# A hybrid decoder trunk: queries and keys of the stick-breaking layers by products of 512 and 256 columns, one PSUM bank per head

## The chip, the core and the metric

The kernel runs as one program on one core of a Trainium2 chip. The metric is the device time of one execution in microseconds (us), the median of a few runs. Five engines work side by side and meet at semaphores: TensorE (PE; its weight loads are listed apart as PEld), VectorE (DVE), ScalarE (ACT), GpSimd (POOL) and SyncE (SP), which here only issues DMAs.

## The reference, cut to what matters

Four layers, T = 256 tokens, width 1024, 8 heads of 128; layers 0 and 3 are stick-breaking, layer 1 differential, layer 2 forgetting attention. A feed-forward net stands before and behind each attention, so there are eight.

```python
for i in range(DEPTH):
    x = x + 0.5 * swiglu(rms_norm(x, norm_g[i, 0]), ...)
    h = rms_norm(x, norm_g[i, 1])
    q, k, v = jnp.split(h @ w_qkv[i], 3, axis=-1)
    if i % 3 == 0:      # stick-breaking, per block of 128 queries
        z = q @ k.T * HEAD_DIM ** -0.5, masked strictly (SB_NEG)
        log_one_minus = log_sigmoid(-z)
        w = exp(z + log_one_minus + rev_excl_cumsum(log_one_minus))
        mix = w @ v
    ...
    x = x + mix @ w_o[i]
    x = x + 0.5 * swiglu(rms_norm(x, norm_g[i, 2]), ...)
return rms_norm(x, final_g)
```

## The kernel before, in words

**Three products for one.** A float32 product is made of three fp32r products: a value is split into a high part (a copy rounded to fp32r) and a low part (the rest). With weights W and tokens X it is W_hi X_hi + W_hi X_lo + W_lo X_hi, summed in PSUM. `product` (lines 1258 to 1262) issues these three.

**The weight stream.** Weights come in chunks of 128 x 2048. For each chunk SP loads it into one of four `raw` buffers, ACT makes the high part (`hi`, line 459, tile `w_hi`) and DVE the low part (`lo`, line 742, tile `w_lo`), both in rings of six. `split_to(c)`, on ACT and on DVE, means: do this for all chunks up to number c. PE waits for `lo_ready` of a chunk before it uses it, and a `raw` buffer is loaded again when `lo` has read it. The tokens (`xg`) are split as well: `xg[:, 0]` is the high part, `xg[:, 1]` the low part, each 8 blocks of 128 rows by 256 tokens.

**An attention layer** has four pairs of heads, j = 0 to 3. `ATT_ORDER` gives the chunks in the order of the stream: v0 v1 q0 k0 v2 v3 q1 k1 q2 k2 o0 q3 k3 o1 o2 o3. `a` is the pair whose scores are made, `b` the pair before it. Nothing schedules the work: each engine runs its own list, written out by hand, in order. For j of 1 to 3 they are these, with the names that the prediction uses:

- PE: `head_projection` of q head 0, q head 1, k head 0 (each 8 times `product`, with 256 columns, into half of a bank: q into bank 0 of `work`, k into bank 1); `mixed(b)` (line 1581 on, the later sums of the log terms); `head_projection` of k head 1; `weighted_values(b)` (line 1600 on, into bank 0); for j = 2 also `output(0)`; `scores(a)` (line 1566 on, into banks 2 and 3).
- DVE: `scale_qk` of q (line 990: PSUM times the row of norms, into `q_t`, one instruction for both heads), `log_weights(b)` (line 1007), `scale_qk` of k, `mix(b)` (line 1013, the low part of the mixed values), `mask(a)` (line 1064), `normalise(a)` (lines 1084 and 1087). Between them stand the `lo` instructions.
- ACT: `hi` instructions, `weights(b)` (lines 596 and 598, the exponentials of both heads), `mix(b)` (line 608), `exponentials(a)` (lines 640, 642, 644 and, behind line 1084 on DVE, 646).

`mixed` waits for line 1087, `weighted_values` for line 596 (head 0) and line 598 (head 1), `scores` for `scale_qk` of k. Behind the last pair PE runs `output(1)`, a quarter of `output(2)`, `mixed(3)`, a quarter of `output(2)`, `weighted_values(3)`, and the rest of the outputs. In pair 0 the value projections `values((2,))` and `values((3,))` stand where `weighted_values` stands later.

Of the kernel before, what the change touches and what calls it, by code (L numbers as in the profile page):

```python
# [14 lines left out]
P = 128  # L15
# [25 lines left out]
DMA_SCRATCH = 8192  # L41
# [7 lines left out]
KINDS = [i % 3 for i in range(DEPTH)]  # L49
LAM_INIT = 0.8 - 0.6 * math.exp(-0.3 * KINDS.index(DIFF))  # L50

# [109 lines left out]
def trunk(nc, stream, x_in, gains, consts, lam_in, subln_in, wf_in, bf_in, final_in, out):  # L161
    with ExitStack() as ctx:
# [29 lines left out]
        pair_h = sb("pair_h", [P, COLS])  # L192
        idle_in = pair_h[:, 0:P]
# [59 lines left out]
        rope_in = sem("rope_in")  # L253

# [108 lines left out]
        def slot_free(eng, c):  # L363

            if c < RING:
                return
            c -= RING
            layer, n, c0, att, no = [p for p in phases() if p[2] <= c][-1]
            what, j = (ATT_ORDER if att else FFN_ORDER)[c - c0]
            if (what, j) in (("down", UNITS - 1), ("o", PAIRS - 1)):  # L370
                eng.wait_ge(acc_ready, BANKS * (n + 1))
            elif what == "top":
                eng.wait_ge(top_used, no * len(PLAIN) + PLAIN.index(j) + 1)
            elif what == "bottom":
                eng.wait_ge(gu_psum, (no * len(PLAIN) + PLAIN.index(j)) * TB + 2)
            elif what == "down":
                eng.wait_ge(down_used, no * (UNITS - 1) + j + 1)
            elif what in PARTS:
                eng.wait_ge(part_psum, (no * len(SEVEN) + SEVEN.index(j)) * len(PARTS) + PARTS.index(what) + 1)
            elif what == "v":  # L380
                eng.wait_ge(v_psum, layer * PAIRS + j // 2 * 2 + 2)
            elif what == "o":
                eng.wait_ge(out_used, layer * (PAIRS - 1) + j + 1)
            else:
                eng.wait_ge(qk_psum, 2 * (layer * PAIRS + j) + (what == "k") + 1)
# [56 lines left out]
        def _(act):  # L442
# [114 lines left out]
            def attention(layer, n, c0, _, kind):  # L557
# [12 lines left out]
                act.preload_act_table_set("natural_log_exp_and_others")  # L570
                values(0)
                values(1)
                if layer == 0:
                    act.wait_ge(lam_psum, 1)
                    nc.scalar.activation(lam_e[:], work[:, 3, 0:2], ACT.Exp).then_inc(lam_exp, 1)
# [4 lines left out]
                if kind == FOX:  # L580

                    act.wait_ge(f_ready, 1)
                    nc.scalar.activation(fg[:, 1], fg[:, 0], ACT.Abs).then_inc(act_step, 1)
                    own_step()
                    nc.scalar.activation(fg[:, 1], fg[:, 1], ACT.Exp, scale=-1.0).then_inc(act_step, 1)
                    own_step()
                    nc.scalar.activation(fg[:, 2], fg[:, 1], ACT.Ln, bias=1.0).then_inc(f_ln, 1)
                values(2)
# [48 lines left out]
                def exponentials(a):  # L637
                    act.wait_ge(scores_ready, a + 1)
                    if kind == STICK:
# [4 lines left out]
                        nc.scalar.activation(s_c, s_b, ACT.Ln, bias=1.0).then_inc(exp_ready, 1)  # L644
                        act.wait_ge(stick_ready, KINDS[:layer].count(STICK) * PAIRS + a - first + 1)
# [9 lines left out]
                for j in range(PAIRS + 1):  # L655
                    a, b = first + j, first + j - 1
                    if j < PAIRS:
# [6 lines left out]
                    if j:  # L664
# [63 lines left out]
        def _(dve):  # L728
            split = [0]
            own = [0]  # L730

# [192 lines left out]
            def attention(layer, n, c0, _, kind):  # L924
# [62 lines left out]
                def scale_qk(dst, bank, count, scale):  # L987

                    dve.wait_ge(qk_psum, count)
# [118 lines left out]
                for j in range(PAIRS + 1):  # L1108
                    a, b = first + j, first + j - 1
                    if j < PAIRS:  # L1110
# [12 lines left out]
                        if kind == STICK or kind == DIFF and j < 2 or kind == FOX and j != 1:  # L1123
                            split_to(q_chunk + 4)
                    if kind == STICK and j in (2, 4):
                        log_weights(b)
                    if j < PAIRS:
                        scale_qk(k_t, 1, 2 * a + 2, 1.0)
# [4 lines left out]
                    if j and kind != DIFF:  # L1133
                        mix(b)
# [14 lines left out]
                    if j < PAIRS:  # L1149
# [5 lines left out]
                        elif kind != DIFF or j == 0:  # L1155
                            split_to(q_chunk + (5 if j else 6))
# [100 lines left out]
        def _(pe):  # L1257
# [227 lines left out]
            def attention(layer, n, c0, _, kind):  # L1485
# [44 lines left out]
                def head_projection(c, bank, h, between=None):  # L1530

                    pe.wait_ge(lo_ready, c + 1)
                    ins = project(work[:, bank, h * T:(h + 1) * T], c, h * P, between)
                    if h:
                        ins.then_inc(qk_psum, 1)
# [119 lines left out]
                for j in range(PAIRS):  # L1655
# [6 lines left out]
                    if not (kind == DIFF and j == 2):  # L1662
                        head_projection(c, 0, 0)
# [3 lines left out]
                    head_projection(c, 0, 1)  # L1667
# [4 lines left out]
                    head_projection(c + 1, 1, 0)  # L1672
# [12 lines left out]
                    head_projection(c + 1, 1, 1, between)  # L1685
                    if j == 0:
# [3 lines left out]
                        pe.wait_ge(qk_ready, 2 * a + 1)  # L1690
# [9 lines left out]
                    if kind != DIFF or j > 1:  # L1700
                        if kind == DIFF:
                            pe.wait_ge(rope_in, 2 * j + 1)
                        else:
# [83 lines left out]
```

## Time and profile before

| | us |
|---|---|
| median of 3 runs | 1895.06 |
| lowest and highest of them | 1894.70, 1895.39 |
| the profiled execution | 1894.82 |
| its span (first to last instruction) | 1893.0 |
| PE busy | 1878.9 (99% of the span) |
| DVE busy | 1536.3 (81%) |
| ACT busy | 1073.7 (57%) |
| granted TensorE clock, mean | 0.999 |
| DMA | 349 MB, 184 GB/s |

The span starts at 0; the attention of layer 0 lies at about 195 to 296 us and that of layer 3 at about 1603 to 1704 us. The profiled execution took 1.82 us more than its span. PE is the engine that is nearly always busy; ends of matmuls are modelled, so what counts for it is the distance from one start to the next.

### The profile page before, as it was taken

How to read it: one execution, taken by the hardware profiler on the slowest of the kernel's cores; microseconds unless marked ns; L12 is line 12 of the kernel's file. 1: busy time of each engine (PE TensorE's matmuls, PEld its weight loads, DVE VectorE, ACT ScalarE, POOL GpSimd, SP SyncE). 2: the span in 40 equal slices, each digit the busy share in tenths (PEclk: the TensorE clock that was granted, in tenths of full speed). 3: DMA queues.
4: the chain of work that ended last, by engine and by line, in shares of the span. 5: the costliest groups of instructions: out<-in, count | busy, mean ns of one | idle time of the engine just before them, and what ended most of it. 6: DMA issues, size and time to landing. Idle time of an engine off the chain costs nothing.

```text
span 1893.0 us, 22572 instructions
## 1 busy us (share of the span) xinstructions
PE 1878.9 (99%) x9408; PEld 1591.6 (84%) x9408; DVE 1536.3 (81%) x1341; ACT 1073.7 (57%) x1107; POOL 19.9 (1%) x34
## 2 busy tenths in 40 slices
PE   9999999999999999999999999999999999999998
PEld 7888998888888898788888889988888888998886
DVE  7987568987898778898799865789879987559985
ACT  6655555655565544665566553466556655556653
POOL 0000000000000000100000000000000000000000
PEclk9999999999999999999999999999999999999999
DMA  6557343456254542344625453434462545433542
GB/s 248 200 230 267 134 156 133 200 200 246 101 226 198 230 168 102 153 200 200 266 110 227 198 200 123 170 131 200 200 267 114 226 196 198 180 132 132 229 198 86
DMA packets 49893, 349.09 MB, mean 184 GB/s; under 512 B 6144, under 2 KB 6400, under 8 KB 7936
## 3 DMA queue, kind: packets, MB, share of 16 engines
q1 hardware_dynamic: 49360, 346.54, 47.2%
q8 instruction: 74, 1.21, 0.3%
q10 hardware_dynamic: 432, 1.11, 0.2%
q14 instruction: 27, 0.22, 0.0%
HBM read 346.58 MB, written 1.05 MB: 184 GB/s over the span
## 4 chain that ended last, share of the span: by engine, by line
PE 89%; DVE 7%; ACT 2%; issue 1%; DMA 0%; POOL 0%; POOLq 0%; ACTq 0%; DVEq 0%
PE work L1260 18%; PE work L1262 18%; PE work L1261 18%; PE acc L1260 10%; PE acc L1262 10%; PE acc L1261 10%; DVE w_lo L742 3%; PE work L1418 1%; PE acc L1304 1%; PE work L1462 1%; PE work L1600 1%; ACT w_hi L459 0%; PE work L1566 0%; DMA x<-x_dram 0%; PE work L1570 0%
## 5 line engine op out<-in xcount | busy, mean ns | idle before, releaser
L742 DVE TENSOR_TENSOR w_lo<-raw,w_hi 128x2048 fp32r<-128x2048 f32 x327 | 741.7, 2284 | 33.6 <-ACT w_hi L459 33.5
L459 ACT ACTIVATE w_hi<-raw 128x2048 fp32r<-128x2048 f32 x327 | 614.1, 1909 | 81.1 <-DVE raw L762 63.3
L1260 PE MATMUL work<-w_hi,xg 128*128 128x512 f32 x1040 | 411.2, 395 | 1.0 <-DVE xg L1185 1.0
L1262 PE MATMUL work<-w_hi,xg 128*128 128x512 f32 x1040 | 405.5, 390 | 0.0
L1261 PE MATMUL work<-w_lo,xg 128*128 128x512 f32 x1040 | 404.8, 389 | 0.0
L1260 PE MATMUL acc<-w_hi,m_hi 128*128 128x512 f32 x824 | 325.6, 395 | 0.2
L1262 PE MATMUL acc<-w_hi,m_lo 128*128 128x512 f32 x824 | 321.2, 390 | 0.0
L1261 PE MATMUL acc<-w_lo,m_hi 128*128 128x512 f32 x824 | 320.9, 389 | 0.0
L1262 PEld LDWEIGHTS work<-w_hi,xg 128*128 128x128 f32 x1040 | 195.3, 188 | 41.5
L1260 PEld LDWEIGHTS work<-w_hi,xg 128*128 128x128 f32 x1040 | 195.3, 188 | 39.4 <-issue 1.2
L1261 PEld LDWEIGHTS work<-w_lo,xg 128*128 128x128 f32 x1040 | 195.5, 188 | 38.4
L1262 PEld LDWEIGHTS acc<-w_hi,m_lo 128*128 128x128 f32 x824 | 154.7, 188 | 32.8
L1260 PEld LDWEIGHTS acc<-w_hi,m_hi 128*128 128x128 f32 x824 | 154.8, 188 | 31.7 <-DVE w_lo L742 1.0
L1261 PEld LDWEIGHTS acc<-w_lo,m_hi 128*128 128x128 f32 x824 | 154.9, 188 | 30.7
L742 DVE TENSOR_TENSOR w_lo<-extra,w_hi 128x2048 fp32r<-128x2048 f32 x72 | 164.2, 2281 | 0.0
L459 ACT ACTIVATE w_hi<-extra 128x2048 fp32r<-128x2048 f32 x72 | 135.3, 1913 | 46.1 <-DVE extra L755 36.7
L1262 PE MATMUL work<-w_hi,wide_r 128*128 128x512 f32 x384 | 149.8, 390 | 0.0
L1260 PE MATMUL work<-xg,w_hi 128*128 128x256 f32 x512 | 148.6, 290 | 0.6 <-DVE fg L955 0.5
L1262 PE MATMUL work<-xg,w_lo 128*128 128x256 f32 x512 | 144.7, 283 | 0.0
L1261 PE MATMUL work<-xg,w_hi 128*128 128x256 f32 x512 | 144.7, 283 | 0.0
L482 ACT ACTIVATE m_hi<-work 128x512 fp32r<-128x512 f32 x88 | 49.8, 595 | 136.3 <-PE work L1418 109.7
L806 DVE TENSOR_TENSOR m_lo<-work,m_hi 128x512 fp32r<-128x512 f32 x88 | 58.3, 686 | 67.4 <-ACT m_hi L482 67.4
(199 smaller groups left out, 2194.1 us busy)
## 6 DMA issues: line engine op xcount, KB each, us to landing
raw<-stream_dram SPq DMA_DIRECT2D x303, 1024.0 KB, 5.0
extra<-stream_dram SPq DMA_DIRECT2D x24, 1024.0 KB, 6.9
x<-x_dram SPq DMA_DIRECT2D x2, 512.0 KB, 8.1
raw<-stream_dram ACTq DMA_DIRECT2D x2, 512.0 KB, 7.7
cst<-consts_dram SPq DMA_DIRECT2D x1, 832.0 KB, 6.4
out_dram<-x SPq DMA_DIRECT2D x3, 256.0 KB, 2.4
final_gain<-final_gain_dram SPq DMA_DIRECT2D x1, 512.0 KB, 6.9
out_dram<-wide SPq DMA_DIRECT2D x1, 256.0 KB, 2.8
```

The lines of the kernel that those rows point to most:

```text
L459: nc.scalar.activation(w_hi[:, c % RING, :], raw_at(place), ACT.Copy).then_inc(hi_ready, 1)
L482: nc.scalar.activation(m_hi[:, u % 2 * 2:u % 2 * 2 + 2, :], halves(hidden_bank(s)), ACT.Copy).then_inc(h_hi_ready, 1)
L742: nc.vector.tensor_tensor(w_lo[:, c % RING, :], raw_at(place), w_hi[:, c % RING, :].bitcast(F32), ALU.subtract).then_inc(lo_ready, 1)
L806: nc.vector.tensor_tensor(m_lo[:, u % 2 * 2:u % 2 * 2 + 2, :], halves(hidden_bank(s)), m_hi[:, u % 2 * 2:u % 2 * 2 + 2, :].bitcast(F32), A ...
L1260: nc.tensor.matmul(dst, a_hi, b_hi, start=start, stop=False, skip_group_check=skip)
L1261: nc.tensor.matmul(dst, a_hi, b_lo, start=False, stop=False, skip_group_check=skip)
L1262: return nc.tensor.matmul(dst, a_lo, b_hi, start=False, stop=stop, skip_group_check=skip)
L1304: ins = nc.tensor.transpose(turned(bank)[:, d, :], x_part(bank)[:, d * P:(d + 1) * P], ident)
L1418: ins = nc.tensor.transpose(hidden_bank(s)[:, t * T + tb * P:t * T + (tb + 1) * P], h[:, t * P:(t + 1) * P], ident)
L1462: ins = nc.tensor.transpose(hidden_bank(s)[:, t * T + tb * P:t * T + (tb + 1) * P], hidden_source(s)[tb][:, t * P:(t + 1) * P], ident)
L1600: nc.tensor.matmul(bank, v[:, 0, cols], w[:, 0:T], start=True, stop=True)
```

## The change

In the stick-breaking layers `packed_projection` takes the place of `head_projection`. For each of the 8 blocks it issues one product of W_hi with both token parts side by side (512 columns: X_hi into the first half of a bank, X_lo into the second) and one of W_lo with X_hi (256 columns, added to the first half). So a head fills a whole bank: head 0 bank 0, head 1 bank 1, for q and then again for k. ACT copies each bank into the new tile `head_halves` (`head_copy`, semaphore `head_copied`); DVE adds the two halves (`heads_joined`) and then scales in place: for q one addition and one scaling over both heads, for k these two for each head. PE waits for the copy of q's head before it makes the same head of k; ACT waits for the addition of q before it copies k, and for all three additions of a pair before it copies the next q.

The lists are rearranged in these layers: on DVE the `lo` that stood between `log_weights` and `scale_qk` of k in pairs 1 and 3 now stands behind `mask`, and the one behind `mask` now stands behind `normalise`; on ACT the `hi` that stood between `weights` and `mix` now stands behind `mix`. `DMA_SCRATCH` is halved, and `qk_psum` now counts heads in all layers.

```diff
+                def packed_projection(j, k, h):
+                    c = c0 + ATT_ORDER.index(("qk"[k], j))
+                    pe.wait_ge(lo_ready, c + 1)
+                    if k:
+                        pe.wait_ge(head_copied, 4 * PACKED.index((layer, j)) + h + 1)
+                    cols = slice(h * P, (h + 1) * P)
+                    for d in range(DT):
+                        high = lambda: nc.tensor.matmul(halves(work[:, h, :]), proj(w_hi, c)[:, d, cols], xg[:, :, d, :],
+                                                        start=d == 0, stop=d == DT - 1, skip_group_check=True)
+                        if d < DT - 1:
+                            high()
+                        ins = nc.tensor.matmul(work[:, h, 0:T], proj(w_lo, c)[:, d, cols], xg_hi[:, d, :],
+                                               start=False, stop=False, skip_group_check=True)
+                    ins = high()
+                    ins.then_inc(qk_psum, 1)
...
+                def head_copy(j, k, h):
+                    i = 2 * PACKED.index((layer, j)) + k
+                    act.wait_ge(qk_psum, 4 * (first + j) + 2 * k + h + 1)
+                    if i:
+                        act.wait_ge(heads_joined, 3 * (i // 2) + (1 if k else 0))
+                    nc.scalar.activation(head_halves[:, h, :], work[:, h, :], ACT.Copy).then_inc(head_copied, 1)
...
+                        for h in range(2) if k else (slice(None),):
+                            dve.wait_ge(head_copied, 2 * (i + k) + (h + 1 if k else 2))
+                            joined[0] += 1
+                            nc.vector.tensor_tensor(dst[:, h], head_halves[:, h, 0:T], head_halves[:, h, T:2 * T],
+                                                    ALU.add).then_inc(heads_joined, 1)
+                            dve.wait_ge(heads_joined, joined[0])
+                            row = r_row[:] if k else both(r_row[:])
+                            ins = nc.vector.scalar_tensor_tensor(out=dst[:, h], in0=dst[:, h], scalar=scale, in1=row,
+                                                                 op0=ALU.mult, op1=ALU.mult)
...
+                    if packed:
+                        head_copy(j, 0, 1)
+                        head_copy(j, 1, 0)
                     if j:
                         weights(b)
+                    if packed:
+                        head_copy(j, 1, 1)
+                        mix(b)
...
                         if kind == STICK and j in (1, 3):
                             log_weights(b)
+                            scale_qk(k_t, 1, 2 * a + 2, 1.0)
+                            mix(b)
...
-                            split_to(q_chunk + (5 if j else 6))
+                            split_to(q_chunk + (6 if j == 0 else 4 if kind == STICK and j in (1, 3) else 5))
```

DVE in layer 0, from behind `mask` of pair 1 to `log_weights` of the next turn, before:

```order
L742 TENSOR_TENSOR w_lo<-raw,w_hi 128x2048 [waits hi_ready]
L1084 SCALAR_TENSOR_TENSOR scratch<-scratch 128x768 [waits exp_ready]
L1087 TENSOR_TENSOR scratch_r<-scratch,scratch_r 128x768 [waits stick_hi_ready]
L990 SCALAR_TENSOR_TENSOR q_t<-work,r_row 128x512 [waits qk_psum]
L742 TENSOR_TENSOR w_lo<-raw,w_hi 128x2048 [waits hi_ready]
L1007 TENSOR_TENSOR scratch<-scratch,work 128x384 [waits mixed_psum]
```

and in the changed kernel, the same place:

```order
L771 TENSOR_TENSOR w_lo<-raw,w_hi 128x2048 [waits hi_ready]
L1127 SCALAR_TENSOR_TENSOR scratch<-scratch 128x768 [waits exp_ready]
L1130 TENSOR_TENSOR scratch_r<-scratch,scratch_r 128x768 [waits stick_hi_ready]
L771 TENSOR_TENSOR w_lo<-raw,w_hi 128x2048 [waits hi_ready]
L1024 TENSOR_TENSOR q_t<-head_halves 128x512 [waits head_copied]
L1028 SCALAR_TENSOR_TENSOR q_t<-q_t,r_row 128x512 [waits heads_joined]
L771 TENSOR_TENSOR w_lo<-raw,w_hi 128x2048 [waits hi_ready]
L1050 TENSOR_TENSOR scratch<-scratch,work 128x384 [waits mixed_psum]
```

Behind line 1130 there now stand two `lo` and two instructions for q ahead of the log weights, where one `lo` and one for q stood.

ACT in layer 0, from behind line 644 of pair 0 to the weights, before:

```order
L646 ACTIVATE scratch_r<-scratch 128x768 [waits stick_ready]
L459 ACTIVATE w_hi<-raw 128x2048 [waits qk_psum,raw_loaded3]
L459 ACTIVATE w_hi<-raw 128x2048 [waits v_psum,raw_loaded0]
L596 ACTIVATE w_t<-scratch 128x384 [waits logw_ready]
L598 ACTIVATE w_t<-scratch 128x384 [waits logw_ready]
```

and in the changed kernel:

```order
L580 ACTIVATE head_halves<-work 128x512 [waits heads_joined,qk_psum]
L667 ACTIVATE scratch_r<-scratch 128x768 [waits stick_ready]
L463 ACTIVATE w_hi<-raw 128x2048 [waits qk_psum,raw_loaded3]
L463 ACTIVATE w_hi<-raw 128x2048 [waits v_psum,raw_loaded0]
L580 ACTIVATE head_halves<-work 128x512 [waits heads_joined,qk_psum] x2
L615 ACTIVATE w_t<-scratch 128x384 [waits logw_ready]
L617 ACTIVATE w_t<-scratch 128x384 [waits logw_ready]
```

The copy of q's head 0 stands ahead of line 667; those of q's head 1 and k's head 0 stand behind the two `hi` instructions and ahead of the weights.

## Rows read from the trace of the kernel before

**Rows 1.** The page: busy time (share) and instructions; granted clock; chain by engine.

```profile
PE 1878.9 (99%) x9408; PEld 1591.6 (84%) x9408; DVE 1536.3 (81%) x1341; ACT 1073.7 (57%) x1107; POOL 19.9 (1%) x34
...
PEclk9999999999999999999999999999999999999999
...
PE 89%; DVE 7%; ACT 2%; issue 1%; DMA 0%; POOL 0%; POOLq 0%; ACTq 0%; DVEq 0%
```

**Rows 2.** Timeline, PE, layer 0: start, duration (us), engine, line, operation, idle before.

```profile
197.37 0.39 PE L1262 MATMUL work<-w_hi,xg 128*128 128x512 f32 x1
...
203.49 0.39 PE L1262 MATMUL work<-w_hi,xg 128*128 128x512 f32 x1
203.72 0.28 PE L1260 MATMUL work<-xg,w_hi 128*128 128x256 f32 x1
...
206.47 0.28 PE L1262 MATMUL work<-xg,w_lo 128*128 128x256 f32 x1
```

**Rows 3.** Groups by shape: line, count, busy us, mean ns, idle before, releaser.

```profile
L527 ACT ACTIVATE scratch<-work 128x512 f32<-128x512 f32 x72 | 42.9, 596 | 122.2 <-PE work L1262 122.2
...
L812 DVE TENSOR_TENSOR wide<-wide 128x512 f32<-128x512 f32 x8 | 5.5, 682 | 0.0
...
L983 DVE TENSOR_TENSOR wide<-cst,work 128x256 f32<-128x256 f32 x8 | 3.3, 415 | 0.0
```

**Rows 4.** Timeline, ACT, layer 0, behind the scores of pair 0.

```profile
232.91 0.84 ACT L646 ACTIVATE scratch_r<-scratch 128x768 fp32r<-128x768 f32 x1 [1.03 <-DVE scratch L1084]
233.66 3.70 ACT L459 ACTIVATE w_hi<-raw 128x2048 fp32r<-128x2048 f32 x2
```

**Rows 5.** Timeline, DVE, layer 0, pairs 1 and 2.

```profile
235.59 2.29 DVE L742 TENSOR_TENSOR w_lo<-raw,w_hi 128x2048 fp32r<-128x2048 f32 x1 [0.84 <-ACT w_hi L459]
237.80 0.68 DVE L990 SCALAR_TENSOR_TENSOR q_t<-work,r_row 128x512 f32<-128x512 f32 x1
238.40 1.01 DVE L1007 TENSOR_TENSOR scratch<-scratch,work 128x384 f32<-128x384 f32 x2
...
241.53 0.68 DVE L990 SCALAR_TENSOR_TENSOR k_t<-work,r_row 128x512 f32<-128x512 f32 x1
...
249.38 0.96 DVE L1087 TENSOR_TENSOR scratch_r<-scratch,scratch_r 128x768 fp32r<-128x768 f32 x1 [0.91 <-ACT scratch_r L646]
250.25 0.69 DVE L990 SCALAR_TENSOR_TENSOR q_t<-work,r_row 128x512 f32<-128x512 f32 x1
```

**Rows 6.** Timeline, PE, PEld and DVE, layer 0, pairs 1 and 2.

```profile
236.71 0.34 PE L1581 MATMUL work<-scratch_r,cst_r 128*128 128x384 f32 x1
...
237.77 0.36 PE L1260 MATMUL work<-xg,w_hi 128*128 128x256 f32 x1
...
240.72 0.60 PE L1600 MATMUL work<-w_t,v 128*128 128x256 f32 x2
...
242.27 0.30 PEld L1566 LDWEIGHTS work<-q_t,k_t 128*128 128x128 f32 x2 [0.26 <-DVE k_t L990]
...
256.23 0.28 PE L1262 MATMUL work<-xg,w_lo 128*128 128x256 f32 x1
...
256.35 0.60 PE L1600 MATMUL work<-w_t,v 128*128 128x256 f32 x2
256.55 0.69 DVE L990 SCALAR_TENSOR_TENSOR k_t<-work,r_row 128x512 f32<-128x512 f32 x1 [1.85 <-PE work L1262]
```

**Rows 7.** Timeline, DVE, ACT and PE, layer 0, behind the last pair.

```profile
285.74 0.96 DVE L1087 TENSOR_TENSOR scratch_r<-scratch,scratch_r 128x768 fp32r<-128x768 f32 x1 [0.91 <-ACT scratch_r L646]
...
288.22 1.02 DVE L1007 TENSOR_TENSOR scratch<-scratch,work 128x384 f32<-128x384 f32 x2 [1.52 <-PE work L1585]
...
288.81 0.53 ACT L596 ACTIVATE w_t<-scratch 128x384 f32<-128x384 f32 x1 [3.10 <-DVE scratch L1007]
...
289.42 0.67 PE L1600 MATMUL work<-w_t,v 128*128 128x256 f32 x2
```

**Rows 8.** Waits, 1650 to 1757 us (layer 3): in total, times, longest.

```profile
PEld work L1566 <- DVE k_t L990: 0.5, 2, 0.3
```

More of the change, by code:

```diff
@@ L40 @@
 RAW = 4
-DMA_SCRATCH = 8192
+DMA_SCRATCH = 4096
 RING = 6
@@ L49 @@
 KINDS = [i % 3 for i in range(DEPTH)]
+PACKED = [(layer, j) for layer in range(DEPTH) for j in range(PAIRS)
+          if KINDS[layer] == STICK]
 LAM_INIT = 0.8 - 0.6 * math.exp(-0.3 * KINDS.index(DIFF))
@@ L384, in slot_free @@
             else:
-                eng.wait_ge(qk_psum, 2 * (layer * PAIRS + j) + (what == "k") + 1)
+                eng.wait_ge(qk_psum, 4 * (layer * PAIRS + j) + 2 * (what == "k") + 2)
         block = ctx.enter_context(nc.Block())
@@ L570, in attention @@
                 act.preload_act_table_set("natural_log_exp_and_others")
+                def head_copy(j, k, h):
[4 more added lines that the diff above has]
+                    nc.scalar.activation(head_halves[:, h, :], work[:, h, :], ACT.Copy).then_inc(head_copied, 1)
                 values(0)
                 values(1)
+                if kind == STICK:
+                    for h in range(2):
+                        head_copy(0, 0, h)
                 if layer == 0:
@@ L587, in attention @@
                     nc.scalar.activation(fg[:, 2], fg[:, 1], ACT.Ln, bias=1.0).then_inc(f_ln, 1)
+                if kind == STICK:
+                    split_to(c0 + ATT_ORDER.index(("v", 3)))
+                    for h in range(2):
+                        head_copy(0, 1, h)
                 values(2)
@@ L656, in attention @@
                     a, b = first + j, first + j - 1
+                    packed = 0 < j < PAIRS and kind == STICK
                     if j < PAIRS:
@@ L730, in _ @@
             own = [0]
+            joined = [0]
             def done(ins):
@@ L1127, in attention @@
                     if j < PAIRS:
-                        scale_qk(k_t, 1, 2 * a + 2, 1.0)
+                        if kind != STICK or j not in (1, 3):
+                            scale_qk(k_t, 1, 2 * a + 2, 1.0)
                         if kind == DIFF:
@@ L1132, in attention @@
                             forget_bias()
-                    if j and kind != DIFF:
+                    if j and kind != DIFF and (kind != STICK or j not in (1, 3)):
                         mix(b)
@@ L1661, in attention @@
                         pe.wait_ge(osq_ready, j - 1) if kind == DIFF else pe.wait_ge(mix_ready, b)
-                    if not (kind == DIFF and j == 2):
+                    packed = (layer, j) in PACKED
+                    if packed:
+                        packed_projection(j, 0, 0)
+                    elif not (kind == DIFF and j == 2):
                         head_projection(c, 0, 0)
@@ L1689, in attention @@
                             forget_bias((0, 1))
-                        pe.wait_ge(qk_ready, 2 * a + 1)
+                        if packed:
+                            pe.wait_ge(head_copied, 4 * PACKED.index((layer, j)) + 3)
+                        else:
+                            pe.wait_ge(qk_ready, 2 * a + 1)
                         values((3,))
```

27 lines of the change are left out of this document (18 added, 9 removed).

## The prediction

> **What bounds the kernel now.** I read the page first: PE is busy for 99% of the span, its clock stands at full in all slices, and PE carries 89% of the chain that ended last [rows 1]. So time is won only where PE's own starts move closer together, and lost wherever PE is made to wait; nothing behind it gives a lost microsecond back, because the feed-forward stages that follow run PE without a break. Then I read PE's timeline for the distance between starts, since its durations overlap. In a run of 512-column products of the fp32r kind, 27 starts lie between 197.37 and 203.49: 0.2267 us each. In a head projection the 24 starts from 203.72 to 206.47 (23 distances) are 0.1196 apart [rows 2]. At 2.4 GHz the columns alone take 0.2133 and 0.1067; so each product, of either width, costs some 0.013 us beyond its columns. Third, I read the timelines of all engines in layer 0's attention to see how late each thing that PE waits for already is. There PE has two waits of 0.26 us on `k_t` ahead of `scores`, in pairs 1 and 3 [rows 6]; layer 3 repeats them [rows 8]. That is the place to watch: the slack is used up before anything is added.
>
> **What PE gains.** A head takes 24 products before, 24 x 0.1196 = 2.87 us, and 8 x 0.2267 + 8 x 0.1196 = 2.77 us after. The columns are the same (6144); only 8 fixed parts are saved, 0.10 us. Two layers have 32 heads: 3.3 us if nothing waits. That is the whole prize, 0.17% of the time. No row shows a 512-column product whose moving operand lies in two pieces 256 columns long, as here. The nearest are the 512-column ones in one piece (0.2267) and two of 256 (0.2392); I take the first, because columns and one fixed part explain both rows, and keep the second (gain 0) for the range.
>
> The row gives 0.013 us for the fixed part. The Trainium skill ("TensorE: Matmul & The Clock Gate", Back-to-back issue gap) puts the gap of a warm product at N/2.4 + 2.5 ns. By that a head would gain only 0.02 us, and the sum below would come to 4.2 us of loss, not 3.2; the trace disagrees, and I go by the trace.
>
> **What is added.** 32 copies on ACT of a bank of 512 columns, 0.60 us each; on DVE, per pair, an addition and a scaling for q (0.68 each, the SBUF addition's row) and two of each for k (0.415 each) [rows 3], in place of two of 0.68. That is 19 us on ACT and about 13 us on DVE. Neither engine is full, so it counts only where one of these stands between PE and its next product. A dependent step starts 0.04 after the one before ends (PE's last product 256.23 + 0.28, then DVE at 256.55), PE starts 0.06 after `k_t` (241.53 + 0.68, then 242.27) [rows 5, 6]. Independent steps on DVE follow 0.08 before the last one's end.
>
> **Pair 0: the gain shows.** ACT and DVE have their slack there: the copies of q are made while PE runs the next head, the copies of k wait for the addition of q behind a `lo`, but PE needs that bank only after the 5.4 us of `values((2,))`, and `scores` comes another 5.4 us later. -4 x 0.10 = **-0.40** per layer. If that cover were gone it would be 0.
>
> **Pair 1.** PE comes to `mixed` 0.31 early, 236.40, and would start k's head 1 at 237.46 instead of 237.77 [rows 6]. But this head now waits for a place of its own: bank 1 is free when ACT has copied q's head 1, and that copy stands in ACT's list behind two `hi`, 233.66 to 237.36 [rows 4]. (The wait written at k's head 1; k's head 0 waits for a copy that fits into the 1.03 us in which ACT waits ahead of line 646 [rows 4], so it costs nothing.) Copy 237.27 to 237.87, PE at 237.93, head done at 237.93 + 2.77 + 0.08 (the changeover, as before: 237.77 + 2.87 to 240.72) = 240.78. The gain is spent.
> Meanwhile on DVE: addition of q from 237.91, scaling from 238.63, log weights from 239.23 instead of 238.40 [rows 5]; from the log weights it is 0.59 to line 596 and 0.61 more to PE [rows 7], 240.43, just in time for 240.78. Then k: PE's last product ends at 240.94, ACT copies until 241.58, DVE adds until 242.04 and scales until 242.49, and `scores` starts at 242.55. Before it was 242.27 [rows 6]: **+0.28**. The `lo` that stood between log weights and k has been taken out of this chain; had it stayed, k's head 0 would come 2.2 us later.
>
> **Pair 2: where the moved `lo` lands.** From `scores` to line 1087 nothing new lies on the path, 249.38 - 242.27 = 7.11 us, so line 1087 starts at 249.66. Now there is `lo` (start 0.87 after it, 250.53, and 2.21 long as from 235.59 to 237.80), addition and scaling of q (252.74, 253.46), the second `lo` (254.06), log weights at 256.27 (the steps are those of [rows 5]). PE's `weighted_values` can start 0.59 + 0.61 later, at 257.47. Before it came at 256.35, 14.08 us after `scores`, on PE's own time; PE is ready 0.40 earlier than that now, 242.55 + 13.68 = 256.23 [rows 6]. It waits 1.24 us: against the old distance **+0.84**. Next late behind it is nothing: `output(0)` (5.4 us) hides the k chain of this pair.
>
> **Pair 3** repeats pair 1 (the order of the lists is the same, and so are the waits [rows 8]): **+0.28**.
>
> **Behind the last pair** the second `lo` stands ahead of the log weights: 285.74 + 0.87 + 2.21 = 288.82 instead of 288.22, where DVE had 1.52 us of idle time [rows 7]. PE started `weighted_values` right on the weights (288.81 + 0.53, then 289.42), so it moves with them: **+0.60**.
>
> **Sum.** -0.40 + 0.28 + 0.84 + 0.28 + 0.60 = +1.60 us per layer, +3.2 for layers 0 and 3. The other layers keep their orders, and the halved DMA scratch and later loads cost nothing: a `raw` buffer freed 3 us later still has 10 us and more until its `hi`. The profiled execution took 1894.82 (span 1893.0 and 1.82 around it), so it would take 1898.0; the median stands 0.24 above it, so 1898.2.
>
> **The rivals.**
> 1. *The products in two pieces run like two products.* Place: every head; price 0.10 us per head, but hidden where ACT or DVE sets PE's next start. Per layer 0 + 0.38 + 0.84 + 0.38 + 0.60 = 2.2, together +4.4: 1899.5, slower than before by more than can be mistaken. It decides once the distance of a 512-256 couple exceeds 0.3464 by about 0.01. For it: no row shows such an operand. Against it: all rows fit columns plus one fixed part.
> 2. *The chains are hidden after all and PE's gain stands,* -3.3: 1891.8. This needs the log weights of pair 2 to be ready 1.2 us earlier than worked out, for example if ACT or DVE overlapped the copy with the additions. Against it: all of them are in-order lists whose steps I took from rows, and in pair 1 there was no slack even before. Half of it (only pair 2 hidden) would give +1.5, or 1896.6.
> 3. *The change does not do what it says*: the order of the built program shows it does, 8 + 8 products per head. I give it nothing.
>
> **How the numbers follow.** What can be told from no change here is about 0.2%, 3.8 us. The forecast has 0.70; its +3.2 lies below that limit by only 0.6, and four waits of two layers, each good to 0.1 us or so, may carry it over: 0.48 same, 0.20 slower, 0.02 faster. Rival 1 has 0.15 (0.12 slower, 0.03 same). Rival 2, whole or half, has 0.15 (0.08 faster, 0.07 same). Together faster 0.10, same 0.58, slower 0.32. The range from 1894.5 to 1900.3 leaves out the whole of rival 2 and a tail above rival 1.
>
> **What would show it.** In PE's timeline couples 0.346 us apart, heads of 2.77 us. PE idle ahead of k's head 1 in pairs 1 and 3, released by an ACT copy, about 0.45 us; ahead of `weighted_values` in pair 2 about 1.2 us, released by line 615 (the first exponential); ahead of `scores` in pairs 1 and 3 about 0.5 us, released by DVE on `k_t`; ahead of the last `weighted_values` about 0.7 us. Attention of both layers 1.6 us longer, everything else as it was. I would be wrong if the couples are not 0.346 apart, if pair 2's `weighted_values` does not wait, or if the clock were granted lower after the new waits; before, it was not lowered anywhere, but no wait like that of pair 2 stands in these layers.

## The result and the profile after

The changed kernel takes 1898.62 us, the median of 18 runs (1898.17 to 1898.98), against 1894.91 for the kernel before in the same comparison (18 runs, 1894.23 to 1895.83): 3.7 us more, a ratio of 1.0019 with a 95% interval of 1.0013 to 1.0026. The prediction was 3.2 us more. The profiled execution has a span of 1896.8 us, 3.8 more than before.

The page of the changed kernel, where it answers to [rows 1]:

```profile
PE 1878.6 (99%) x9152; PEld 1578.1 (83%) x9152; DVE 1549.3 (82%) x1373; ACT 1090.7 (58%) x1139; POOL 19.9 (1%) x34
...
PEclk9999999999999999999999999999999999999999
...
PE 88%; DVE 8%; ACT 3%; issue 1%; DMA 0%; POOL 0%; POOLq 0%; ACTq 0%; DVEq 0%
```

PE has 256 instructions fewer, DVE 13 us and ACT 17 us more. PE's share of the chain that ended last has fallen by one point, DVE's and ACT's have risen by one point each. The granted clock stands as before (mean 0.999). The added work by shape (changed kernel: line, count, busy us, mean ns, idle before):

```profile
L1589 PE MATMUL work<-xg,w_hi 128*128 128x512 f32 x256 | 91.7, 402 | 0.5
...
L580 ACT ACTIVATE head_halves<-work 128x512 f32<-128x512 f32 x32 | 18.6, 589 | 23.2 <-DVE q_t L1024 12.6 <-PE work L1589 10.6
...
L1028 DVE SCALAR_TENSOR_TENSOR k_t<-k_t,r_row 128x256 f32<-128x256 f32 x16 | 6.8, 425 | 0.5
L1024 DVE TENSOR_TENSOR k_t<-head_halves 128x256 f32<-128x256 f32 x16 | 6.7, 421 | 3.3 <-ACT head_halves L580 3.3
```

PE's timeline, changed kernel, layer 0, head by head. First the couples, which answer to [rows 2]:

```profile
203.52 0.39 PE L1589 MATMUL work<-xg,w_hi 128*128 128x512 f32 x1
203.74 0.28 PE L1593 MATMUL work<-xg,w_lo 128*128 128x256 f32 x1
203.86 0.40 PE L1589 MATMUL work<-xg,w_hi 128*128 128x512 f32 x1
...
205.63 0.40 PE L1589 MATMUL work<-xg,w_hi 128*128 128x512 f32 x1
```

A couple is one product of 512 columns and one of 256. Here six couples take 2.11 us, 0.352 each. Then the four places that [rows 6, 7] showed before, in all engines' timelines:

```profile
235.06 2.29 DVE L771 TENSOR_TENSOR w_lo<-raw,w_hi 128x2048 fp32r<-128x2048 f32 x1 [0.85 <-ACT w_hi L463]
236.74 0.57 ACT L580 ACTIVATE head_halves<-work 128x512 f32<-128x512 f32 x1
236.95 0.38 PE L1646 MATMUL work<-scratch,cst 128*128 128x128 f32 x2
237.34 0.69 DVE L1024 TENSOR_TENSOR q_t<-head_halves 128x512 f32<-128x512 f32 x1
...
237.42 0.19 PEld L1589 LDWEIGHTS work<-xg,w_hi 128*128 128x128 f32 x1 [0.28 <-DVE w_lo L771]
...
241.64 0.42 DVE L1028 SCALAR_TENSOR_TENSOR k_t<-k_t,r_row 128x256 f32<-128x256 f32 x1
...
242.11 0.30 PEld L1627 LDWEIGHTS work<-q_t,k_t 128*128 128x128 f32 x2 [0.49 <-DVE k_t L1028]
242.12 0.48 PE L1627 MATMUL work<-q_t,k_t 128*128 128x256 f32 x1 [0.30 <-DVE k_t L1028]
...
253.63 2.28 DVE L771 TENSOR_TENSOR w_lo<-raw,w_hi 128x2048 fp32r<-128x2048 f32 x1
...
255.69 0.40 PE L1589 MATMUL work<-xg,w_hi 128*128 128x512 f32 x1
255.83 1.01 DVE L1050 TENSOR_TENSOR scratch<-scratch,work 128x384 f32<-128x384 f32 x2
...
256.41 0.52 ACT L615 ACTIVATE w_t<-scratch 128x384 f32<-128x384 f32 x1 [2.73 <-DVE scratch L1050]
...
257.08 0.45 PE L1661 MATMUL work<-w_t,v 128*128 128x256 f32 x1 [1.00 <-ACT w_t L615]
```

In order of time: k's head 1 starts only after a copy on ACT that ends at 237.31 (236.74 + 0.57); `scores` waits 0.49 us for `k_t`; in pair 2 PE has issued its last product at 255.69 and `weighted_values` cannot start before 257.08, because the log weights (line 1050) stand behind a `lo` that ends at 255.91. Behind the last pair the log weights come late once more, by less:

```profile
290.00 1.01 DVE L1050 TENSOR_TENSOR scratch<-scratch,work 128x384 f32<-128x384 f32 x2
...
290.59 0.52 ACT L615 ACTIVATE w_t<-scratch 128x384 f32<-128x384 f32 x1 [3.69 <-DVE scratch L1050]
...
291.16 0.48 PE L1661 MATMUL work<-w_t,v 128*128 128x256 f32 x1 [0.38 <-ACT w_t L615]
```

Read from PE's starts, layer 0 splits up as in the table. It gives the us from one mark to the next; a mark is the start of PE's first product of that work.

| stretch | before | after | difference | predicted |
|---|---|---|---|---|
| q head 0 of pair 0 to `scores` | 23.06 | 22.73 | -0.33 | -0.40 |
| pair 1: `scores` to `scores` | 15.49 | 15.87 | +0.38 | +0.28 |
| pair 2: `scores` to `weighted_values` | 14.08 | 14.96 | +0.88 | +0.84 |
| `weighted_values` to `scores` | 6.79 | 6.87 | +0.08 | 0 |
| pair 3: `scores` to `scores` | 15.49 | 15.87 | +0.38 | +0.28 |
| `scores` to the last `weighted_values` | 10.79 | 11.34 | +0.55 | +0.60 |
| from there to the last mark | 7.38 | 7.41 | +0.03 | 0 |
| sum | 93.08 | 95.05 | +1.97 | +1.60 |

The last mark is the first output product behind the four short products that bring part of x into `acc` (296.80 before, 298.57 after). Over the same marks layer 3 goes from 92.86 to 94.76, +1.90. The two sums make 3.87. Outside these marks this execution is 0.20 us shorter ahead of layer 0's attention, 0.10 shorter between the two attentions and 0.18 longer behind the second, which gives the 3.8 of the spans. So the halved `DMA_SCRATCH` and the later loads cost nothing there that can be told.

### The profile page after: what moved, and what is told of

It reads as the page before. It is cut to its first block, busy times and chain, and to the rows that moved or that the text cites. A ratio compares the mean times of both kernels' runs of the same rounds, so it can differ in the third digit from the quotient of the medians.

```text
span 1896.8 us, 22170 instructions
## 1 busy us (share of the span) xinstructions
PE 1878.6 (99%) x9152; PEld 1578.1 (83%) x9152; DVE 1549.3 (82%) x1373; ACT 1090.7 (58%) x1139; POOL 19.9 (1%) x34
## 4 chain that ended last, share of the span: by engine, by line
PE 88%; DVE 8%; ACT 3%; issue 1%; DMA 0%; POOL 0%; POOLq 0%; ACTq 0%; DVEq 0%
PE work L1306 17%; PE work L1308 17%; PE work L1307 17%; PE acc L1306 9%; PE acc L1308 9%; PE acc L1307 9%; DVE w_lo L771 3%; PE work L1589 1%; PE work L1464 1%; PE acc L1350 1%; PE work L1508 1%; PE work L1593 1%; PE work L1661 1%; ACT w_hi L463 0%; PE work L1627 0%
## 5 line engine op out<-in xcount | busy, mean ns | idle before, releaser
L771 DVE TENSOR_TENSOR w_lo<-raw,w_hi 128x2048 fp32r<-128x2048 f32 x327 | 741.5, 2283 | 40.4 <-ACT w_hi L463 40.2
L771 DVE TENSOR_TENSOR w_lo<-extra,w_hi 128x2048 fp32r<-128x2048 f32 x72 | 164.2, 2281 | 0.0
L531 ACT ACTIVATE scratch<-work 128x512 f32<-128x512 f32 x72 | 42.9, 596 | 122.2 <-PE work L1308 122.2
L1589 PE MATMUL work<-xg,w_hi 128*128 128x512 f32 x256 | 91.7, 402 | 0.5
L1308 PEld LDWEIGHTS work<-w_hi,wide_r 128*128 128x128 f32 x384 | 72.1, 188 | 15.4
```

What stands on the lines that cost most here:

```text
L531: nc.scalar.activation(place, work[:, bank, :], ACT.Copy).then_inc(part_copied, 1)
L771: nc.vector.tensor_tensor(w_lo[:, c % RING, :], raw_at(place), w_hi[:, c % RING, :].bitcast(F32), ALU.subtract).then_inc(lo_ready, 1)
L1308: return nc.tensor.matmul(dst, a_lo, b_hi, start=False, stop=stop, skip_group_check=skip)
L1589: high = lambda: nc.tensor.matmul(halves(work[:, h, :]), proj(w_hi, c)[:, d, cols], xg[:, :, d, :], start=d == 0, stop=d == DT - 1, skip_g ...
```

## The experiments

Each kernel was timed in five rounds against the kernel before, except one with a single run, marked below. Differences are of medians. The intervals of single ratios are about plus or minus 0.0009 (1.7 us), so a difference of 1 us is read from the timelines, and the time only has to agree. In the timelines of one kernel the same stretch in pairs 1 and 3 and in layers 0 and 3 agrees to 0.04 us.

**Pair 2's wait taken away.** The log weights ahead of the second `lo`:

```diff
+                        if kind == STICK and j == 2:
+                            log_weights(b)
                         if kind == STICK and j not in (1, 3) or kind == DIFF and j < 2 or kind == FOX and j != 1:
                             split_to(q_chunk + 4)
-                    if kind == STICK and j in (2, 4):
+                    if kind == STICK and j == 4:
                         log_weights(b)
```

> The changed kernel with one move: in pair 2 VectorE makes the log weights ahead of the second low part of a weight chunk, not behind it. Theory (the four new waits of a layer carry the loss): the log weights then start at 253.6 instead of 255.8 us, the exponentials are ready before PE ends k's head 1, so the wait of 1.15 us ahead of weighted_values in pair 2 goes, in both layers: 2.2 to 2.3 us less than the changed kernel, 1.4 to 1.5 us above the kernel before (ratio 1.0008). Rival (the loss lies in slower products or in the load of ScalarE and VectorE as such): as the changed kernel, 3.7 us above the kernel before.

Measured: 1896.35 against 1894.63, +1.7. DVE and PE in its timeline:

```profile
253.27 0.69 DVE L1028 SCALAR_TENSOR_TENSOR q_t<-q_t,r_row 128x512 f32<-128x512 f32 x1
253.88 1.01 DVE L1050 TENSOR_TENSOR scratch<-scratch,work 128x384 f32<-128x384 f32 x2
254.81 2.28 DVE L771 TENSOR_TENSOR w_lo<-raw,w_hi 128x2048 fp32r<-128x2048 f32 x1
...
255.93 0.40 PE L1591 MATMUL work<-xg,w_hi 128*128 128x512 f32 x1
...
256.17 0.38 PE L1663 MATMUL work<-w_t,v 128*128 128x256 f32 x1
```

`weighted_values` follows the last product without a wait, 13.81 us after `scores` (242.36) instead of 14.96. The other stretches stay. So this wait is 1.15 us a layer, 2.3 us of the 3.7. The rival, that the added load as such costs the time, falls: the load is the same here.

**PE's part undone.** Each product of 512 columns cut into two of 256, all else as in the changed kernel:

```diff
-                        high = lambda: nc.tensor.matmul(halves(work[:, h, :]), proj(w_hi, c)[:, d, cols], xg[:, :, d, :],
-                                                        start=d == 0, stop=d == DT - 1, skip_group_check=True)
+                        def high():
+                            nc.tensor.matmul(work[:, h, 0:T], proj(w_hi, c)[:, d, cols], xg_hi[:, d, :],
+                                             start=d == 0, stop=d == DT - 1, skip_group_check=True)
+                            return nc.tensor.matmul(work[:, h, T:2 * T], proj(w_hi, c)[:, d, cols], xg_lo[:, d, :],
+                                                    start=False, stop=d == DT - 1, skip_group_check=True)
```

> The changed kernel with its products of 512 columns cut into two of 256 (24 products a head as before, into the same halves of the same banks; copies, additions and all waits as in the changed kernel). Theory (most of PE's gain is swallowed by waits set by ScalarE and VectorE): only pair 0 (4 heads) and k's head 1 in pairs 1 and 3 show the longer heads, 6 of 16 heads a layer, 0.06 to 0.1 us each: 0.7 to 1.2 us above the changed kernel, 4.4 to 4.9 us above the kernel before. Rival (PE's gain counts in full): 16 heads a layer, 2.0 to 3.3 us above the changed kernel, 5.7 to 7.0 above the kernel before.

Measured: 1899.44 against 1894.63, +4.8. In the timelines the layers are 2.42 and 2.40 us longer than before, against 1.97 and 1.90 in the changed kernel, so the merged products are worth 0.95 us. In pair 1 three heads take 8.71 us, as before the change, and 8.55 with merged products, 0.053 a head; in pair 0 a head gains 0.08. For 32 heads that would be 1.9 us (8 of 0.08 and 24 of 0.053). Half of it is swallowed: in pair 1 `scores` to `scores` is 15.91 with the longer heads and 15.87 with the shorter, because PE's next start is set by ACT and DVE.

**ScalarE's copy moved between the two `hi`.**

```diff
                         q_chunk = c0 + ATT_ORDER.index(("q", j))
-                        split_to(q_chunk + 4)
-                    if packed:
-                        head_copy(j, 0, 1)
+                        if packed:
+                            split_to(q_chunk + 3)
+                            head_copy(j, 0, 1)
+                        split_to(q_chunk + 4)
+                    if packed:
                         head_copy(j, 1, 0)
```

> The changed kernel with one move: ScalarE copies q's head 1 between the two high parts of weight chunks, not behind both. Theory: the copy is done at 235.5 instead of 237.3 us, PE starts k's head 1 right behind mixed (0.43 us sooner, in pairs 1 and 3), and since the chain to k_t hangs on the end of that head, scores come 0.4 us sooner too: 1.6 us less than the changed kernel in the two layers, 2.1 us above the kernel before (ratio 1.0011). Rival (scores waits for the slower VectorE chain, the sum of q and the log weights, whatever PE does): no change, 3.7 us above the kernel before.

Measured: 1897.41 against 1894.63, +2.8, and in the timelines 0.69 and 0.64 us a layer less than the changed kernel (1.3 in all, where 1.6 was expected). ACT, PEld and PE of pair 1:

```profile
232.94 1.90 ACT L463 ACTIVATE w_hi<-raw 128x2048 fp32r<-128x2048 f32 x1
234.75 0.57 ACT L580 ACTIVATE head_halves<-work 128x512 f32<-128x512 f32 x1
235.22 1.90 ACT L463 ACTIVATE w_hi<-raw 128x2048 fp32r<-128x2048 f32 x1
...
236.87 0.19 PEld L1591 LDWEIGHTS work<-xg,w_hi 128*128 128x128 f32 x1
236.90 0.48 PE L1591 MATMUL work<-xg,w_hi 128*128 128x512 f32 x1
```

k's head 1 starts 10.84 us after the scores before it (226.06), without a wait, where it took 11.20. It also settles a label. In the changed kernel the trace puts this wait down to `w_lo` on DVE (L771), whose instruction ends at 237.35; the copy ends at 237.31. Here the same `w_lo` instruction runs from 234.88 to 237.17, and PE starts at 236.87, ahead of its end. So PE did not wait for it; what it had waited for was the copy.

**The moving operand in one piece.** A layout of `xg` in which high and low part of a block are neighbours:

```diff
-        xg = sb("xg", [P, 2, DT, T], F32R)
+        xg = sb("xg", [P, DT, 2, T], F32R)
...
-        xg_hi, xg_lo = xg[:, 0], xg[:, 1]
+        xg_hi, xg_lo = xg[:, :, 0], xg[:, :, 1]
...
-                        high = lambda: nc.tensor.matmul(halves(work[:, h, :]), proj(w_hi, c)[:, d, cols], xg[:, :, d, :],
+                        high = lambda: nc.tensor.matmul(halves(work[:, h, :]), proj(w_hi, c)[:, d, cols], xg[:, d],
```

> The changed kernel with the two token parts of a block side by side in SBUF, so that the moving operand of a product of 512 columns is one piece of 512 columns and not two of 256. In the changed kernel a couple of 512 and 256 columns takes 0.348 to 0.353 us, not the 0.3464 of the rows before. If the two pieces are the cause: couples of 0.3464 us, 0.2 us less a layer, 3.3 us above the kernel before. If the other engines' traffic or the alternation of widths is the cause: couples of 0.35 as before, 3.7 us above.

Measured: 1898.66 against 1894.63, +4.0; in the timelines +1.92 and +1.96 a layer, as in the changed kernel. Three heads take 8.55 us in pair 1, as there (in one of six places, layer 0's pair 2, 8.47). So two pieces of 256 columns cost nothing against one of 512 that can be told here. That was the prediction's first rival; the last experiment on the widths, below, says the same.

**The order alone.** The kernel before, with only DVE's list rearranged:

```diff
                         if kind == STICK and j in (1, 3):
                             log_weights(b)
+                            scale_qk(k_t, 1, 2 * a + 2, 1.0)
+                            mix(b)
-                        if kind == STICK or kind == DIFF and j < 2 or kind == FOX and j != 1:
+                        if kind == STICK and j not in (1, 3) or kind == DIFF and j < 2 or kind == FOX and j != 1:
...
-                            split_to(q_chunk + (5 if j else 6))
+                            split_to(q_chunk + (6 if j == 0 else 4 if kind == STICK and j in (1, 3) else 5))
```

> The kernel before with only VectorE's list rearranged as in the change (in pairs 1 and 3 the low part of a weight chunk stands behind the mask instead of ahead of k's scaling, and the one behind the mask stands behind line 1087); no packed products, no copies, no additions. From the rows of before: k_t is ready ahead of PE in pairs 1 and 3, so the waits of 0.26 us go (-0.3 each); pair 2's log weights come 13.0 us after scores (7.11 + 0.87 + 2.21 + 0.60 + 2.21), weighted_values 14.2 after, where PE comes at 14.08 (+0.1); the last ones 0.6 later (+0.6). Sum +0.1 a layer: within 0.5 us of the kernel before. Theory: the moves alone are harmless, it is the copy and the additions in these chains that make pair 2 wait 1.2 us. Rival: the moves alone make most of the loss, 2 to 3 us above the kernel before.

Measured: 1895.42 against 1894.85, +0.6. PE behind the last pair:

```profile
277.91 0.60 PE L1569 MATMUL work<-q_t,k_t 128*128 128x256 f32 x2
...
289.16 0.70 PE L1603 MATMUL work<-w_t,v 128*128 128x256 f32 x2 [0.41 <-ACT w_t L596]
```

In layer 0, pairs 1 and 3 take 15.26 each (-0.23), pair 2 14.31 (+0.23), and from the last `scores` to the last `weighted_values` it is 11.25 (+0.46); +0.25 together. So the moved `lo` cost time at both places by themselves, and win nearly as much back ahead of `scores`. Behind the last pair they make most of the changed kernel's 0.55; in pair 2 they make 0.23 of its 0.88, and the rest comes with the copy and the addition.

**Three moves at once.** The first and the third experiment together, and the last `lo` behind the last log weights. The third of these moves:

```diff
                     if kind == STICK and j == 4:
                         log_weights(b)
+                        split_to(c0 + ATT_CHUNKS)
...
                         normalise(a)
-                        split_to(q_chunk + 5)
+                        if not (kind == STICK and j == 3):
+                            split_to(q_chunk + 5)
```

> The changed kernel with three moves: log weights of pair 2 ahead of the second low part; the last low part behind the last log weights; q's head 1 copied between the two high parts. Theory: the three waits go together, since each stands on its own chain: pair 0 -0.33, pairs 1 and 3 0.0 each, pair 2 -0.25, behind the last pair 0: -0.5 a layer, 1 us below the kernel before (ratio 0.9995). Rival (taking one wait away makes the next thing late): 0 to 1.5 us above the kernel before.

Measured: 1893.77 against 1894.85, -1.1 (ratio 0.9995, 0.9986 to 1.0004). In the timelines -0.63 a layer against the kernel before: `weighted_values` in pair 2 comes 13.73 after `scores`, the last `weighted_values` is back at 10.79 behind its `scores`, pairs 1 and 3 stand at 15.51. So these three waits add up and can be taken away one by one; a wait of 0.30 us for `k_t` ahead of `scores` stays. The interval of the ratio holds 1, so that this kernel is faster than the one before rests on the timelines.

**The two widths in two groups.** All eight products of 512 columns, then all eight of 256:

```diff
                     for d in range(DT):
                         high = lambda: nc.tensor.matmul(halves(work[:, h, :]), proj(w_hi, c)[:, d, cols], xg[:, :, d, :],
...
-                        if d < DT - 1:
-                            high()
...
+                        high()
+                    for d in range(DT):
                         ins = nc.tensor.matmul(work[:, h, 0:T], proj(w_lo, c)[:, d, cols], xg_hi[:, d, :],
...
-                    ins = high()
```

> The changed kernel with the products of a head in another order: all eight of 512 columns, then all eight of 256, instead of in turns. If taking turns of widths is what makes a couple 0.351 us long instead of 0.3464, a head takes 2.78 us instead of 2.82, which shows in pair 0 and in k's head 1 of pairs 1 and 3: 0.4 us less than the changed kernel in all, 3.5 above the kernel before. If it is not: couples cost the same, 3.9 above.

Measured: 1899.43 against 1894.85, +4.6, no gain in the time. (Four of the eleven runs lie at 1898.4 to 1898.7, the profiled one among them, and seven at 1899.4 to 1899.9; the timeline, +1.90 and +1.92 a layer, is of the first kind, and what makes the second is not shown.) The timeline shows part of what was expected: three heads take 8.47 instead of 8.55, most of it where nothing waits for it. PE in pair 1:

```profile
230.47 2.00 PE L1589 MATMUL work<-xg,w_hi 128*128 128x512 f32 x8
232.31 1.12 PE L1593 MATMUL work<-xg,w_lo 128*128 128x256 f32 x8
233.26 2.00 PE L1589 MATMUL work<-xg,w_hi 128*128 128x512 f32 x8
```

Eight of 512 columns take 1.84 us, eight of 256 take 0.95. The eight of 512 are not evenly apart. The sixth starts at 231.63 (a window that begins later shows it), so the first five distances take 1.16 us, 0.232 each, and the last three 0.68, 0.227 each as in [rows 2]. In q's head 0 of pair 0, which follows a run of 512 columns, all eight are 0.227 apart. And the kernel before shows the same where value products of 512 columns follow a head's products of 256 (its PE timeline, line, operation, tiles):

```profile
215.75 0.28 PE L1262 MATMUL work<-xg,w_lo 128*128 128x256 f32 x1
215.87 0.40 PE L1260 MATMUL work<-w_hi,xg 128*128 128x512 f32 x1
...
217.03 0.39 PE L1262 MATMUL work<-w_hi,xg 128*128 128x512 f32 x1
...
218.39 0.39 PE L1262 MATMUL work<-w_hi,xg 128*128 128x512 f32 x1
```

Five distances from 215.87 to 217.03 are 0.232 each, the next six, to 218.39, 0.227. So some 0.03 us is lost behind a change from 256 to 512 columns, and nothing further on. (In a few heads seven distances are long, not five.) With one change a head, three heads gain 0.24 us against plain products, 0.08 a head; in turns they gain 0.16. Both together, grouped and in one piece, in a single run:

> The changed kernel with both: products in two groups by width, and the moving operand of 512 columns in one piece. Grouped alone, the eight products of 512 columns are 0.230 us apart, the eight of 256 0.119. If the two pieces cost the difference to 0.2267, they are now 0.2267 apart and three heads take 8.38 us with their changeover instead of 8.47. If not (any 512-column product with the stationary weights of these chunks is as long while ScalarE and VectorE are busy), 0.230 and 8.47 stay. The total moves by less than 0.3 us either way; the timeline decides, not the time.

Measured: 1.84 us for eight again (249.18 to 251.02), 8.47 for three heads. The 0.003 us per product above [rows 2] is therefore not the pieces and not the turns; it is the distances behind the change of width.

In turns the couples of the changed kernel have two lengths, which the mean of 0.352 hides. In 9 of the 32 heads they are 0.3465 us apart, the sum of the two distances of [rows 2] (209.90 to 211.63 are five couples, 1.73 us), in the other 23 0.353. The load of the other engines does not decide it: in the head from 203.52, with couples of 0.352, DVE does nothing, and in the head from 1647.30, with couples of 0.3465, DVE is busy all the time and ACT half of it. What decides it is not shown.

**Fewer additions in the chain.** With the three moves, k's head 1 of pairs 1 to 3 by 24 plain products and straight from PSUM into `k_t`:

```diff
+                    if k and h and j:
+                        project(work[:, 1, 0:T], c, P).then_inc(qk_psum, 1)
+                        return
...
+                            if h == 1 and pair > first:
+                                dve.wait_ge(qk_psum, 4 * pair + 4)
+                                ins = nc.vector.scalar_tensor_tensor(out=dst[:, 1], in0=work[:, 1, 0:T], scalar=scale,
+                                                                     in1=r_row[:], op0=ALU.mult, op1=ALU.mult)
+                                continue
...
-                        head_copy(j, 1, 1)
                         mix(b)
```

> As the kernel with three moves (e6_moves), and k's head 1 of pairs 1 to 3 is made by 24 plain products of 256 columns and scaled straight from PSUM: no copy, no addition behind it. Theory: what is left of the loss is that copy and addition hang between the end of that head and scores (1.8 us, against the 1.3 us of weighted_values). Without them scores follows weighted_values without a wait in pairs 1 and 3: 0.4 us less each; pair 2's first product then waits up to 0.25 us for the low part of the mixed values. Against the kernel before: pair 0 -0.33, pair 1 -0.2, pair 2 -0.17, pair 3 -0.4: -1.1 a layer, 2.2 us below it (ratio 0.9988). Rival (VectorE is the bound there, not the chain behind k's head 1): no better than e6_moves.

Measured: 1892.31 against 1894.85, -2.5, ratio 0.9987 (0.9978 to 0.9996), the only one of these kernels whose interval lies wholly below 1. The gain is 0.13% of the time. Its timeline at the scores of pair 1 and at pair 2's first product:

```profile
241.16 0.38 PE L1685 MATMUL work<-w_t,v 128*128 128x128 f32 x2
...
241.38 0.60 PE L1650 MATMUL work<-q_t,k_t 128*128 128x256 f32 x2
...
242.96 0.19 PEld L1612 LDWEIGHTS work<-xg,w_hi 128*128 128x128 f32 x1 [0.29 <-DVE m_lo L1072]
```

`scores` comes 15.09 us after the scores before, 0.40 sooner than in the kernel before, with no wait for `k_t`. The next thing late is the low part of the mixed values, 0.29 us, where 0.25 was expected. Layer 0 is 1.14 us shorter than before, layer 3 1.12.

**How much of that is the order.** The kernel before with VectorE's list rearranged and the last `lo` behind the last log weights, without packed products:

> The kernel before (no packed products) with VectorE's list rearranged as in the change and its last low part behind the last log weights. From e4_order's timeline (scores to scores 15.26 instead of 15.49 in pairs 1 and 3, pair 2 +0.23, the last turn +0.56) and with the last term gone: -0.2 a layer, 0.4 to 0.5 us below the kernel before (ratio 0.9998). Then what e10_hybrid gains beyond it, 2 us, is due to the packed products. Rival: the rearranged lists make all of e10_hybrid's 2.5 us, and the packed products nothing.

Measured: 1894.17 against 1894.92, -0.7 (0.9988 to 1.0006), -0.33 a layer in the timelines. So of the 2.3 us that the hybrid gains in the timelines 0.7 come from an order that needs no packed product at all, and 1.6 from the packed products and what goes with them. Among the latter is one more move of order, the log weights of pair 2 ahead of the second `lo`: here `weighted_values` still comes 14.33 us after `scores`, 0.25 later than in the kernel before. That move was not run without packed products, so up to 0.5 us of the 1.6 may be order as well.

## Why the prediction was right, and where its sizes were off

- **What bounds the kernel.** Right: PE's starts set the time, and nothing gave a lost microsecond back. The difference of the spans is that of the two attention stages.
- **What PE gains.** 0.10 us a head was forecast; 0.08 came in pair 0 (-0.33 for four heads instead of -0.40) and 0.053 in pair 1. The term that was too large is the couple at 0.3464 us, the sum of two distances each read in a run of equal widths. Couples take 0.3465 in 9 heads and 0.353 in 23. The trace of the kernel before already held a warning: five longer distances where 512 columns follow 256 (from 215.87 us). The reason that the text held ready, the operand in two pieces, is not it. The fixed part of a product, 0.013 us by the rows, is borne out where a width stays the same. By the 2.5 ns of the Trainium skill ("TensorE: Matmul & The Clock Gate", Back-to-back issue gap) the merging would have gained 0.02 us a head, and the trace disagrees. The Trainium skill gives that figure there for a product by itself, and says of a stream of weight loads and products, as here, that both set the distance.
- **Pairs 1 and 3.** Right in mechanism: the copy behind two `hi`, then the chain behind k's head 1, both shown by moving them. +0.28 forecast, +0.38 measured. PE starts 0.11 us after the copy where 0.06 was taken from `k_t`, and from k's head 1 to `weighted_values` it takes 2.90 where 2.85 was taken; `scores` then follows 1.77 us behind, as worked out.
- **Pair 2.** Right: two `lo` and two steps for q ahead of the log weights. 14.92 us from scores to `weighted_values` worked out, 14.96 measured, and PE would have been ready at 13.81, not 13.68, for the reason in the second point. The first experiment shows the whole of it. From `weighted_values` behind the wait to the next `scores` it takes 0.08 more, which the sum left out.
- **Behind the last pair.** +0.60 forecast, +0.55 measured, for the reason given: the order alone makes +0.46 there, and the `lo` moved behind the log weights brings it to nothing.
- **The waits.** Forecast 0.45 us ahead of k's head 1, 1.2 in pair 2, 0.5 ahead of `scores` and 0.7 ahead of the last `weighted_values`. Measured: 0.36 (11.20 against 10.84), 1.15, 0.49, and 0.65 (11.34 against the 10.69 of the last experiment).
- **Sum.** 1.60 a layer forecast, 1.97 and 1.90 measured. Of the missing 0.3 to 0.4 some 0.2 are the two pairs, 0.07 pair 0 and 0.1 pair 2 with its restart. Each term was good to 0.1 us, as the text said, but all of them except the last erred to the same side.
- **Rivals.** The first (two pieces run like two products) gave 4.4 us and lies within the interval (2.5 to 4.9 us), so the time alone cannot tell it from the forecast; the one-piece experiment excludes its cause. The second (the waits are hidden) did not come about; it is what the moves make of the kernel afterwards.
- **The middle.** The measured 3.7 us is 0.19%, on the near side of what was called no change, by 0.1 us. The interval of the ratio, 1.0013 to 1.0026, reaches over that limit, so the side is in part luck; the waits and their sizes are not luck.

## What to carry to other kernels

Where one engine is busy all the time and the others feed it through in-order lists, the gain of fewer instructions counts only where that engine is not already waiting: read the slack of each thing it waits for before adding a step to the chain that makes it. A chain through such a list also waits for the unrelated work that the list puts into it, here two weight splits of 2.2 us ahead of the log weights; moving one of them by one place gave back more than half of the loss. And a packed product whose halves must be added elsewhere paid where its result was needed late, and not in the last head ahead of the scores: making that head by plain products took off another 1.0 us in the timelines.

## What the runs showed of the hardware

- Products of the fp32r kind, with a stationary block loaded for each, are 0.2267 us apart at 512 columns and 0.1196 at 256 in a run of one width. Behind a change from 256 to 512 columns the first five distances are 0.232 on average (216 us of the kernel before, 230 us of the grouped one), in a few places seven or more are long. In turns of the two widths a couple takes 0.3465 in some heads and 0.353 in most.
- A moving operand in two pieces of 256 columns costs the same as one in one piece: grouped, eight products take 1.84 us and three heads 8.47 us either way.
- A wait can be put down to the wrong releaser: the trace named a VectorE instruction that ended at 237.35 us for a wait that a ScalarE copy, ended at 237.31, had caused; moving the copy alone took it away.
- The gap in pair 2 of the changed kernel (PE's starts at 255.69 and 257.08, 1.00 us idle by the modelled ends) did not lower the granted clock: it is 1.00 from 256 to 258 us and from 258 to 262, the full level of 2.4 GHz.
